# First attention of a two-block model: values stationary, the result laid out by feature

## The reference

```python
# 8 heads of 64 in 2 groups of 4; per query t and head, three softmax branches
p_cmp = masked_softmax(qb @ kc_g, valid_c)      # 31 compressed keys
p_slc = masked_softmax(qb @ kg, smask)          # selected blocks; topk covers all 8, so all keys up to t
p_win = masked_softmax(qb @ kw, wmask)          # window of 512: all keys up to t
out = gates[0] * (p_cmp @ vc) + gates[1] * (p_slc @ vg) + gates[2] * (p_win @ vw)   # sigmoid gates
mix = concatenate([y_ret, y_nsa]) @ w_out       # y_ret: a retention of 4 heads of 128
```

## Time and profile before

| | us | share of the span |
|---|---|---|
| median of three runs | 1913.14 | |
| the profiled execution | 1912.61 | |
| its span | 1910.8 | |
| TensorE busy (PE) | 1856.8 | 97% |
| VectorE busy | 1139.7 | 60% |
| ScalarE busy | 735.9 | 39% |
| GpSimd busy | 175.7 | 9% |
| first attention, from 176.4 to 286.8 us | 110.4 | 6% |

### The profile page before, as it was taken

One profiled execution on the slowest core, in us unless ns is written; L12 is line 12 of the kernel. 1 busy time (PEld: TensorE's weight loads), 2 busy tenths in 40 slices (PEclk: granted clock), 3 DMA queues, 4 the chain that ended last, 5 costly groups with the idle time before them and its releaser, 6 DMA issues.

```text
span 1910.8 us, 24681 instructions
## 1 busy us (share of the span) xinstructions
PE 1856.8 (97%) x8914; PEld 1513.4 (79%) x8914; DVE 1139.7 (60%) x1625; ACT 735.9 (39%) x1077; POOL 175.7 (9%) x181
## 2 busy tenths in 40 slices
PE   8999989999999999999999999999999999999998
PEld 6788778888888887887788888888666688888887
DVE  7767654784774778777543434476777554334344
ACT  6355222542432444554432322343544342323232
POOL 0020000300000011010000000002467300000000
PEclk9999999999999999999999999999999999999999
...
DMA packets 48216, 165.68 MB, mean 87 GB/s; under 512 B 5376, under 2 KB 7424, under 8 KB 48000
## 3 DMA queue, kind: packets, MB, share of 16 engines
...
...
## 4 chain that ended last, share of the span: by engine, by line
PE 86%; DVE 8%; ACT 2%; issue 2%; POOL 1%; DMA 0%; SPq 0%; DVEq 0%; ACTq 0%; POOLq 0%
PE ps L625 26%; PE ps L627 25%; PE ps L626 25%; PE ps L883 2%; PE ps L986 2%; DVE w_lo L2077 1%; POOL x L538 1%; ACT w_hi L1441 1%; PE ps L847 1%; PE ps L1241 1%; DVE tmp L2114 1%; PE ps L956 1%; PE ps L868 0%; DVE qk_c L2799 0%; PE ps L816 0%
## 5 line engine op out<-in xcount | busy, mean ns | idle before, releaser
L1441 ACT ACTIVATE w_hi<-raw 128x1024 fp32r<-128x1024 f32 x280 | 296.7, 1060 | 779.5 <-PE ps L627 779.3
L625 PE MATMUL ps<-h_hi,w_hi 128*128 128x512 f32 (+1 forms) x1288 | 509.3, 395 | 10.1 <-DVE w_lo L2352 7.2
L626 PE MATMUL ps<-h_lo,w_hi 128*128 128x512 f32 (+1 forms) x1288 | 500.0, 388 | 0.0
L627 PE MATMUL ps<-h_hi,w_lo 128*128 128x512 f32 (+1 forms) x1288 | 499.9, 388 | 0.0
L2077 DVE TENSOR_TENSOR w_lo<-raw,w_hi 128x1024 fp32r<-128x1024 f32 x280 | 345.0, 1232 | 120.6 <-ACT w_hi L1441 119.0
L625 PEld LDWEIGHTS ps<-h_hi,w_hi 128*128 128x128 f32 x1288 | 243.2, 189 | 64.6 <-DVE w_lo L2352 7.2
L627 PEld LDWEIGHTS ps<-h_hi,w_lo 128*128 128x128 f32 x1288 | 243.0, 189 | 50.6
L626 PEld LDWEIGHTS ps<-h_lo,w_hi 128*128 128x128 f32 x1288 | 243.1, 189 | 49.5 <-issue 2.0
L625 PE MATMUL ps<-hid_hi,w_hi 128*128 128x512 f32 (+1 forms) x716 | 273.6, 382 | 1.8 <-DVE w_lo L2077 0.9
L627 PE MATMUL ps<-hid_hi,w_lo 128*128 128x512 f32 (+1 forms) x716 | 272.6, 381 | 0.0
L626 PE MATMUL ps<-hid_lo,w_hi 128*128 128x512 f32 (+1 forms) x716 | 272.6, 381 | 0.0
...
## 6 DMA issues: line engine op xcount, KB each, us to landing
...
```

Source lines behind the costliest of these rows:

```text
L625: nc.tensor.matmul(out, a[0], b[0], start=start, stop=False)
L626: nc.tensor.matmul(out, a[0], b[1], start=False, stop=False)
L627: return nc.tensor.matmul(out, a[1], b[0], start=False, stop=stop)
L1441: nc.scalar.activation(w_high(panel, i), raw[:, panel % 4, :], ACT.Copy).then_inc(w_hi_ready, 1)
```

## The change

The values become stationary and the weights moving, as in the second attention. `block_values` issues two matmuls of 64 x 256: two heads' 256 columns go to partitions 0 to 63, the other two heads' to partitions 64 to 127. The result lies by feature, so the transposes by token, and the tile `by_token`, go; the rows of `w_out` are laid out in the new order by the host. The column of ones is gone from `nv` and `vc`. The softmax sums come in two ways: for the compressed block from two more matmuls with ones, for the two large branches from GpSimd, which adds the weights of a branch (`add_block`, 24 additions of 128x512, from unit 2 on), and then four matmuls with ones (`unit_sums`), which stand behind the values of the next unit's third block. VectorE turns sums into shares by two 32x32 transposes around a reciprocal, once for the compressed branch (`compressed_result`, at the unit's first block) and once for the others (`unit_result`), and adds the three branches (`unit_add`). ScalarE rounds (`unit_rounded`), and GpSimd takes the rest (`unit_rest`, 7 of the 8 units; VectorE the last). The gates are laid out by feature once (`spread_gates`, at the start).

The order is written for two blocks at a time: scores of the next two blocks, with the rounds of maxima behind each, then the values of the present two. `pr` has six tiles. ScalarE's splits of the first two output panels move from ahead of the attention into unit 5, VectorE's `low` for them from behind unit 5 to units 6 and 7.

```diff
...
+PROBS = 6
...
-            pr = sb("pr", [P, 4, S], F32, cc)
-            by_token = sb("by_token", [P, 2, 4, P], F32, cc)
-            term = sb("term", [P, 3, 4, 64], F32, cc)
...
+            pr = sb("pr", [P, PROBS, S], F32, cc)
+            term = sb("term", [P, 2, 3, 256], F32, cc)
+            unit_out = sb("unit_out", [P, 2, 256], F32, cc)
...
-        count, turns = len(nsa[n + 2]["rounds"]), len(nsa[n]["blocks"]) - 1
-        return nsa[n + 2]["rounds"][count * (b - 1) // turns:count * b // turns]
+        count, turns = len(nsa[n + 2]["rounds"]), len(nsa[n]["blocks"])
+        return nsa[n + 2]["rounds"][count * b // turns:count * (b + 1) // turns]
...
+        def add_block(m):
+            u, b = flat[m]
+            n, w = u["n"], u["blocks"][b]
+            if w["s"] == 0 or w["kt"] == 0:
+                return
+            if w["kt"] == 1 and n >= 2:
+                pool.wait_ge(unit_totals, n)
+            pool.wait_ge(block_exp, m + 1)
+            total = block_sum(n, w["s"])
+            nc.gpsimd.tensor_tensor(total, prob(m - 2) if w["kt"] == 1 else total, prob(m), ALU.add).then_inc(unit_added, 1)
+            pool.wait_ge(unit_added, last_add(m))
...
+        for m in range(NSA_BLOCKS):
+            add_block(m)
+            for u in nsa[1:]:
+                if m == u["first"] + 10:
+                    unit_rest(u["n"] - 1)
+        unit_rest(NSA_UNITS - 2)
...
+        def unit_sums(u):
+            n = u["n"]
+            if u["qt"]:
+                pe.wait_ge(unit_added, adds_before[n + 1])
+            pe.wait_ge(unit_taken, bank_one["taken"])
+            pe.wait_ge(low_spread, bank_one["spread"])
+            for s in (1, 2):
+                moving = block_sum(n, s) if u["qt"] else prob(u["first"] + s)
+                for a in range(2):
+                    last = nc.tensor.matmul(ps[64 * a:64 * a + 64, 1, cols_of(s - 1)], ones[:, 0:64], moving[:, cols_of(a)],
+                                            start=True, stop=True)
+            last.then_inc(unit_totals, 1)
...
             pe.wait_ge(block_exp, m + 1)
-            if b == 0 and u["n"]:
-                pe.wait_ge(sum_taken, u["n"])
+            if b == 0 and n:
+                pe.wait_ge(compressed_taken, n)
+            if b == 0 and n == NSA_UNITS - 1:
+                pe.wait_ge(mix_ready, 2)
+            if b == 1 and n >= 2:
+                pe.wait_ge(sum_taken, n - 1)
             v = vc[:, g, :] if w["s"] == 0 else nv[:, w["kt"], w["s"] - 1, g, :]
-            for h in range(4):
-                n = 4 * w["s"] + h
-                last = nc.tensor.matmul(ps[:, 6 + n // 6, n % 6 * 65:n % 6 * 65 + 65], pr[:, m % 4, h * P:(h + 1) * P], v,
-                                        start=w["kt"] == 0 and n in (0, 6), stop=w["last"], skip_group_check=True)
+            bank, at = (6 + n % 2, cols_of(w["s"] - 1)) if w["s"] else (0, cols_of(0))
+            for a in range(2):
+                last = nc.tensor.matmul(ps[64 * a:64 * a + 64, bank, at], v, prob(m)[:, cols_of(a)], start=w["kt"] == 0 and w["s"] < 2,
+                                        stop=w["last"], skip_group_check=True)
+            if b == 0:
+                for a in range(2):
+                    last = nc.tensor.matmul(ps[64 * a:64 * a + 64, 0, cols_of(1)], ones[:, 0:64], prob(m)[:, cols_of(a)], start=True,
+                                            stop=True, skip_group_check=True)
             last.then_inc(block_pv, 1)
...
+        for m in range(2):
+            block_scores(*flat[m])
+        turn_low(nsa[1])
+        for m in range(0, NSA_BLOCKS, 2):
+            for k, (u, b) in enumerate(flat[m:m + 2]):
+                if m + 2 + k < NSA_BLOCKS:
+                    block_scores(*flat[m + 2 + k])
+                if u["n"] + 2 < NSA_UNITS:
+                    for r in rounds_at(u["n"], b):
+                        best_round(nsa[u["n"] + 2], r)
+            for u in nsa[2:]:
+                if m == turned_at(u["n"]):
+                    turn_low(u)
+            for u, b in flat[m:m + 2]:
                 block_values(u, b)
+            if m == 0:
+                spread_gates()
+            for u, b in flat[m:m + 2]:
+                n = u["n"]
+                if b == 2 and n:
+                    unit_sums(nsa[n - 1])
                 if n >= NSA_UNITS - 2 and b in (2, 5):
...
+                    pe.wait_ge(compressed_taken, n + 1)
                     ret_widen(2 * (n - NSA_UNITS + 2) + b // 3)
...
+        unit_sums(nsa[-1])
...
-            pe.wait_ge(mix_ready, 4 + NT - 1 + half)
+            pe.wait_ge(mix_ready, 4 + 4 * half)
+            if half:
+                pe.wait_ge(unit_low, NSA_UNITS - 1)
...
+        def unit_rounded(n):
+            act.wait_ge(unit_sum, n + 1)
+            nc.scalar.activation(unit_tiles(h_hi, nsa[n]), unit_out[:, n % 2, :].rearrange("p (j q) -> p j q", j=2), ACT.Copy).then_inc(unit_high, 1)
...
+        for m in range(NSA_BLOCKS):
+            act.wait_ge(block_s, m + 1)
+            if m >= PROBS:
+                u, b = flat[m - PROBS]
+                act.wait_ge(block_pv, m - PROBS + 1)
+                if last_add(m - PROBS):
+                    act.wait_ge(unit_added, last_add(m - PROBS))
+                elif b:
+                    act.wait_ge(unit_totals, u["n"] + 2)
+            nc.scalar.activation(prob(m), ps[:, 4 + m % 2, :], ACT.Exp, scale=0.125).then_inc(block_exp, 1)
+            for u in nsa[1:]:
+                if m == u["first"] + 8:
+                    unit_rounded(u["n"] - 1)
+            if m in (nsa[-3]["first"] + 2, nsa[-3]["first"] + 4):
+                split(OUT1 + (m - nsa[-3]["first"]) // 2 - 1)
...
+        def compressed_result(u):
+            n, w = u["n"], w24[:, 0:8]
+            totals, shares = tmp[:, 1, 0:256], tmp[:, 1, 256:S]
+            dve.wait_ge(block_pv, u["first"] + 1)
+            link(V.transpose(totals, ps[:, 0, 256:S]))
+            link(V.scalar_tensor_tensor(w, totals[:, 0:256:32], 1e-30, gate_at(u, 0, 1)[:, 0, :], ALU.max, ALU.mult))
+            link(V.reciprocal(w, w))
+            link(V.transpose(shares, w.unsqueeze(2).to_broadcast([P, 8, 32])))
+            signal(V.tensor_tensor(term[:, n % 2, 2, :], ps[:, 0, 0:256], shares, ALU.mult), compressed_taken, wait=False)
...
         def unit_result(u):
+            n, w = u["n"], w24[:, 8:24]
+            totals, shares = sq[:, 0, :], sq[:, 1, :]
+            dve.wait_ge(unit_totals, n + 2)
+            signal(V.transpose(totals, ps[:, 1, :]), unit_taken)
+            link(V.scalar_tensor_tensor(w.rearrange("p (s c) -> p s c", s=2), totals[:, 0:S:32].rearrange("p (s c) -> p s c", s=2), 1e-30,
+                                        gate_at(u, 1, 3), ALU.max, ALU.mult))
+            link(V.reciprocal(w, w))
+            link(V.transpose(shares, w.unsqueeze(2).to_broadcast([P, 16, 32])))
             dve.wait_ge(block_pv, u["first"] + len(u["blocks"]))
...
+            signal(V.tensor_tensor(term[:, n % 2, 0:2, :].rearrange("p s c -> p (s c)"), ps[:, 6 + n % 2, :], shares, ALU.mult), sum_taken)
+        def unit_add(n):
+            dve.wait_ge(compressed_taken, n + 1)
+            t = unit_out[:, n % 2, :]
+            if n >= 2:
+                dve.wait_ge(unit_low, n - 1)
+            link(V.tensor_tensor(t, term[:, n % 2, 0, :], term[:, n % 2, 1, :], ALU.add))
+            signal(V.tensor_tensor(t, t, term[:, n % 2, 2, :], ALU.add), unit_sum)
...
+        for m in range(0, NSA_BLOCKS, 2):
+            for u, b in flat[m:m + 2]:
+                if u["n"] + 2 < NSA_UNITS:
+                    for r in rounds_at(u["n"], b):
+                        largest(nsa[u["n"] + 2], r)
+                    if b == len(u["blocks"]) - 1:
+                        lowest(nsa[u["n"] + 2])
+            for u in nsa[2:]:
+                if m == turned_at(u["n"]):
+                    spread_low(u)
...
+            for u, b in flat[m:m + 2]:
+                n = u["n"]
+                if b == 0:
+                    compressed_result(u)
+                if b == 2 and n:
+                    unit_result(nsa[n - 1])
+                    unit_add(n - 1)
+                if n == NSA_UNITS - 2 and b == 1:
+                    ret_diagonal(0)
                 if n >= NSA_UNITS - 2 and b in (2, 5):
                     h = 2 * (n - NSA_UNITS + 2) + b // 3
                     ret_finish(h)
                     if h < 3:
                         ret_diagonal(h + 1)
-            if n + 2 < NSA_UNITS:
-                lowest(nsa[n + 2])
-            if n == NSA_UNITS - 3:
-                ret_diagonal(0)
-                low(OUT1)
-                low(OUT1 + 1)
+                if n >= NSA_UNITS - 2 and b == 7:
+                    low(OUT1 + n - NSA_UNITS + 2)
...
```

157 lines of the change are left out of this document (70 added, 87 removed).

## The result

The changed kernel takes **1926.87 us** (median of four runs, 1924.93 to 1928.99) where the kernel before took 1911.37 beside it. The ratio is 1.0083, with a 95% interval of 1.0068 to 1.0098: 15.5 us slower, clear of noise. The forecast was 1916, with a range that ended at 1924. The profiled execution took 1925.8 us (1912.6 before), with a span of 1924.0 (1910.8).

What follows compares the result with a forecast made beforehand. TensorE was taken to bound the first attention, with holes near its end. 1912.6 - 11.0 (own work) - 9.8 (old waits) - 3.3 (old half clock) + 19.9 (new waits) + 6.6 (half clock) + 1.1 (GpSimd) = 1916.1, forecast 1916, range 1897 to 1924.

Steps and rivals of the forecast that it cites:

- TensorE's own work: First attention: cheaper value matmuls and dropped transposes, less the added ones matmuls, make TensorE's work 11.0 us less.
- the halves run side by side: Value matmuls: two blocks take 1.05 us; the rival that they don't adds 21 us, 1937, chance 0.03.
- the score matmul behind them needs 0.32 us to its successor, where behind another score matmul it needs 0.23, so each block costs 0.09 more: Score matmul after a block's values in the old kernel: 0.09 us extra per block, counted within the saving.
- The old waits: TensorE's waits for `term`, an exponential and `by_token` in the first attention, together 9.8 us, would go.
- The walk: Pair-by-pair count of TensorE's new waits behind VectorE's lumps (its chain and sums for a unit) and at retention roots: 19.9 us.
- VectorE's 18.0 of 31.2 us become some 23 for two units, still below TensorE: First attention: VectorE's work grows by 21 us in all, but it stays less busy than TensorE.
- GpSimd beside VectorE: VectorE operations reading two SBUF tiles run a third longer beside GpSimd's additions: 2.2 us, 1.1 on the path.
- The clock: After long waits TensorE runs at half clock: four new stretches cost 6.6 us, and 3.3 us of old ones go.
- VectorE and the clock feed each other: Rival: half clock follows each of seven lumps, 12 us instead of 6.6, plus 3 us of waits; 1924, chance 0.2.
- Absorbed lumps: Rival: only half of the new waits (10 us) and one half-clock stretch come; 1901, chance 0.27.
- the waits at the retention roots: Last two units: TensorE waits 3.7 us at the second head's root and 1.7 at the last, for diagonals behind lumps.
- The signs named for being right: 1.05 us per two blocks, round waits over 8, root wait 3 to 4, half-clock stretches, VectorE +21, GpSimd +40.

Runs made afterwards that it cites:

- e3: The changed kernel with VectorE doing the retention finish and next diagonal ahead of the previous unit's chain and sums in the last two units; 1928.7 us.
- e6: The changed kernel with only the retention finish's first operation and the next diagonal ahead of the previous unit's chain in the last two units; 1927.6 us.
- e8: e7 with GpSimd's 20 additions of units 4 to 7 cut to 8 columns, sums not right; ratio 0.9977 to the kernel before.
- e1: The changed kernel with GpSimd's 20 additions of units 4 to 7 cut from 512 to 8 columns, sums not right; 1923.2 us.
- e11: The changed kernel with eight extra copies of a score matmul in each of seven block pairs, ahead of rounds that wait for VectorE; 1919.0 us.
- e5: The changed kernel with VectorE's product and two sums of a unit moved one pair of blocks later, kept in order; 1912.4 us.
- e12: e7 with the four retention diagonals made by ScalarE instead of VectorE, roots in their old places; ratio 1.0018 to the kernel before.
- e7: The changed kernel with e5's later product and sums, and the next retention diagonal behind a finish's first operation; 1911.4 us.

## Why the prediction was wrong

**TensorE's own work: −11.0 forecast, −4 to −5 measured.** The durations were right. Two blocks' values take 0.92 us (265.17 to 266.09) and the change back 0.1, where 1.05 was forecast for both, so the halves run side by side: that rival is out. What failed is "the score matmul behind them needs 0.32 us to its successor, where behind another score matmul it needs 0.23, so each block costs 0.09 more". The first score matmul of a block takes 0.31 to 0.34 us to its successor behind new values (264.05 to 264.38) and behind rounds (194.47 to 194.78); only straight behind another block's scores it takes 0.24 (264.61 to 264.85), and 9 of the 48 blocks stand so now where 8 did before. So 48 x 0.09 = 4.3 us weren't there to save. And the step from the scores into the 64-column values costs 0.1 more than the one before (0.32 from 264.85 to 265.17 against 0.23 from 261.93 to 262.16), 2.2 us for 24 pairs, which the sum left out. −11.0 + 4.3 + 2.2 = −4.5.

**The old waits: right.** The 9.8 us of waits are gone. Whether their half clock would have gone with them can't be told beside the new.

**The places of the new waits: right; two sizes wrong.** The walk named them one by one. Behind unit 0's sums it gave 2.2 us and 2.9 came, unit 2 had 0.9 and 1.7 (0.7 and 1.9 forecast), unit 5 3.4 (2.3). But the second retention root waited 5.5 us, not 3.7, and the last 4.8, not 1.7. In sum it was 12.2 us for the maxima, where the walk had 12.5, and 10.8 at the roots, where it had 5.4. A wait for GpSimd's sums, of which it took none, came once, with 0.3 us.

**"VectorE's 18.0 of 31.2 us become some 23 for two units, still below TensorE": right for the middle (23.75 of 33.32), wrong where it mattered.** It was never worked out for the last two units, which have the retention as well. There, with the 6 us ahead of them, VectorE is busy 41.20 of 52.38 us. The walk charged each wait as if the rest could be caught up; e3 and e6 show that it can't.

**GpSimd beside VectorE: rightly feared, and sized at a third of what it is or less.** The forecast took a third more on operations with two SBUF tiles, 1.1 us in all. Measured were 3.4 to 3.7 us of the program's time (e8, and e1 by the medians; 5 by e1's ratio). The weight rest that gave the third (1631 against 1232 ns) is a mean over five, and a mean hides a block: an operation that meets an addition stands for the rest of it, up to 1.3 us, however short it is itself. Of the rule in the Trainium skill's GPSIMD Engine Reference, section Key points, I used one half, instructions with two SBUF inputs. Its other half, instructions in a mode with two ports, I left out, and the cast at L2179, with one SBUF tile in, went from 426 ns to 1.37 us in the changed kernel and 1.54 in e6: the trace agrees.

**The clock: the mechanism right, the number of stretches wrong.** Four of 3.4 us were forecast; there were five pieces of 27.2 us together, three of them 6.8 long. They cost 11 us by the ledger, and e11, which took away 19.8 of 26.6 us at half clock, got 7 to 8 back. The rival "VectorE and the clock feed each other" came nearest, with 1924. Its sizes for half clock (12, measured 11) and for the waits (19.9 + 4 − 9.8 = 14.1, measured 13.6) were right. That it came so near is luck all the same: it shares the −11.0 of own work, 6 us too much, and 3 us came back behind the stage that no case had. And the feeding itself is not shown: in e11 the half clock went, and the waits fell by no more than the work put into them.

**Absorbed lumps: out.** That the lumps cost so much was a matter of their place: e5 has the same work and is 14 us faster.

**The steps that failed** are so, in the forecast's own terms: the saving in TensorE's own work (−11.0, some −4.7 measured), the half clock (+6.6, 11.0 measured) and the waits at the retention roots (5.4, 10.8 measured). The signs named for being right came, some of them larger than named, but none of them weighed the saving in TensorE's own work.

What stays open: the 4.4 us of e12 over e7 hold what ScalarE's queue did and the clock (7.4 against 2.0 us at half). In the profiled executions the stage is 2.5 us longer and the waits only 0.4, which points at the clock, but no run separates the two. And e7's stage has TensorE's work some 2 us shorter by the ledger and 5 us more waits than before; no run found out whether the last of these can go.
